# A hybrid FFN and gated-DeltaNet layer on one core: requests, joins and block copies around the first scans in another order

## The reference, cut to what matters

```python
def mix_heads(q, k, v, g, beta, s0):            # per head and direction, per chunk
    a_low = where(strict, einsum(kb, kc) * decay, 0.0)
    sol = triangular_solve(eye + a_low, rhs)    # rhs = [v*beta, k*beta*exp(gc)]
    u_val, w_kd = split(sol)
    def step(S, xs):
        v_new = u_i - w_i @ S
        o = (q_i * exp(g_i)) @ S + qk_i @ v_new
        S = S * exp(g_last) + (k_i * exp(g_last - g_i)).T @ v_new
        return S, o
def pool_mixer(u, w_pool, pool_scale):          # centred window means, a linear map per group
    p = stack([window_mean(u, w) - u for w in (2, 4, 8, 16)])
    return einsum('blgc,gcd->blgd', p, w_pool) * pool_scale
# y = concat([pool_mixer(...), gate(norm(o), z)]) @ w_out
```

## Time and profile before

| | us |
|---|---|
| median of 3 runs (2853.35 to 2856.04) | 2854.99 |
| the profiled execution | 2856.5 |
| its span, first to last instruction | 2854.6 |
| TensorE matmuls busy (98% of the span) | 2799.8 |
| VectorE busy (57%) | 1616.8 |
| ScalarE busy (35%) | 989.9 |
| POOL busy (8%) | 220.8 |

### The profile page before, as it was taken

The page is one execution under the profiler, slowest core; times in us unless marked ns, Lnnn a source line. Parts: engine busy times, 40 slices in busy tenths (PEclk is TensorE's granted clock), DMA queues, the critical chain, the costliest instruction groups (busy, mean ns, idle before and its releaser), DMA issues. The chain is left out here.

```text
span 2854.6 us, 41614 instructions
## 1 busy us (share of the span) xinstructions
PE 2799.8 (98%) x15400; PEld 2357.2 (83%) x15400; DVE 1616.8 (57%) x2080; ACT 989.9 (35%) x1451; POOL 220.8 (8%) x373
## 2 busy tenths in 40 slices
PE   6999999999999999999999999999999999999998
PEld 4688888888888888888888888878988888888887
DVE  4567767677677752223226766745675555555444
ACT  3222222222222221111214555544354444444443
POOL 0000000000000000000101103555120000000001
PEclk9999999999999999999999999999999999999999
DMA  9866677677988956655563666685456666666664
GB/s 369 308 207 221 199 222 221 203 223 250 317 310 304 317 183 201 193 184 171 193 195 97 172 197 182 206 262 171 155 180 191 190 191 191 191 191 192 190 190 144
DMA packets 410340, 604.67 MB, mean 212 GB/s; under 512 B 52960, under 2 KB 303840, under 8 KB 401520
## 3 DMA queue, kind: packets, MB, share of 16 engines
q1 hardware_dynamic: 361824, 419.52, 47.5%
q10 hardware_dynamic: 48400, 183.63, 19.0%
HBM read 560.02 MB, written 43.02 MB: 211 GB/s over the span
## 5 line engine op out<-in xcount | busy, mean ns | idle before, releaser
L2003 DVE TENSOR_TENSOR wl<-raw,wh 128x1024 fp32r<-128x1024 f32 x638 | 784.8, 1231 | 927.2 <-ACT wh L1523 926.5
L1523 ACT CAST wh<-raw 128x1024 fp32r<-128x1024 f32 x638 | 667.7, 1048 | 1455.4 <-PE ps L785 929.9
L783 PE MATMUL ps<-x,wh 128*128 128x512 f32 (+1 forms) x2312 | 903.1, 391 | 0.1
L785 PE MATMUL ps<-x,wl 128*128 128x512 f32 (+1 forms) x2312 | 897.7, 388 | 0.0
L784 PE MATMUL ps<-x,wh 128*128 128x512 f32 (+1 forms) x2312 | 897.6, 388 | 0.0
L783 PEld LDWEIGHTS ps<-x,wh 128*128 128x128 f32 x2312 | 435.0, 188 | 96.1 <-issue 8.9
L785 PEld LDWEIGHTS ps<-x,wl 128*128 128x128 f32 x2312 | 434.7, 188 | 89.9
L784 PEld LDWEIGHTS ps<-x,wh 128*128 128x128 f32 x2312 | 435.1, 188 | 87.3
L2195 DVE SCALAR_TENSOR_TENSOR acc<-abuf,cT,acc 128x1024 f32<-128x1024 f32 x300 | 371.2, 1278 | 19.2 <-DMA abuf<-in_w_ada 18.9
L791 PE MATMUL ps<-x,wh 128*128 128x512 f32 x1408 | 349.2, 393 | 2.6 <-DVE x L2073 2.6
L791 PEld LDWEIGHTS ps<-x,wh 128*128 128x128 f32 x1408 | 254.3, 189 | 48.6 <-issue 2.9
(11 more groups left out here) (309 smaller groups left out, 2346.2 us busy)
## 6 DMA issues: line engine op xcount, KB each, us to landing
raw<-in_ffn_w_in SPq DMA_DIRECT2D x704, 256.0 KB, 3.2
raw<-in_ffn_w_out SPq DMA_DIRECT2D x176, 512.0 KB, 3.6
abuf<-in_w_ada ACTq DMA_DIRECT2D x64, 1024.0 KB, 7.1
abuf<-in_w_ada ACTq DMA_DIRECT2D x96, 512.0 KB, 3.9
x<-d_h ACTq DMA_DIRECT2D x80, 512.0 KB, 3.2
ada_t<-in_ada SPq DMA_DIRECT2D x64, 512.0 KB, 9.3
raw<-in_w_in SPq DMA_DIRECT2D x128, 256.0 KB, 3.5
raw<-in_w_out SPq DMA_DIRECT2D x32, 512.0 KB, 4.5
```

Source lines behind the costliest of these rows:

```text
L783: mm(out, ah, bh, start=first, stop=False, skip_group_check=reopened)
L785: return mm(out, al, bh, start=False, stop=last, skip_group_check=reopened)
L1523: nc.scalar.copy(wh[:, t % HL, :], raw[:, t % RAW, :]).then_inc(hi_done, 1)
L2003: tt(tl, raw[:, t % RAW, :], th.bitcast(F32), ALU.subtract).then_inc(lo_done, 1)
```

## The change

Six things move; no product is added or taken away.

1. SP requests `UF` of head 1 (`level_rows(1)`) ahead of output tiles 0 and 1.
2. In the second pooling set, ScalarE does the join's copy or negation of a step ahead of that step's weight split, and VectorE its negation.
3. In scan 1 VectorE does `fill(0)`, the low part `yl` of pooling group 0, behind `out_mean(0)` and ahead of `state(0)`, where it stood behind `out_gate(0)`.
4. `place` can do its GI half (`"g"`) and its FI half (`"f"`) apart. The GI half ends with a wait for its own copies.
5. `LANE_STEPS` of the second batch has five parts for three: columns 16 to 30 are cut in 16 to 21, 22 to 24 and 25 to 30.
6. POOL's order in the scans: before, columns 16 to 30 came behind `out_power(0)` and ahead of `place(3)`. Now come columns 16 to 21, the GI half of `place(3)`, columns 22 to 24, the FI half, `out_power(1)`, columns 25 to 30. The semaphore `xl_zero` is called `pool_wrote`, and also counts the GI half.

```diff
-LANE_STEPS = (((0, 11), (11, 21), (21, BLK - 1)), ((0, 4), (4, 16), (16, BLK - 1)))
+LANE_STEPS = (((0, 11), (11, 21), (21, BLK - 1)), ((0, 4), (4, 16), (16, 22), (22, 25), (25, BLK - 1)))
...
             set_load(0)
+            level_rows(1)
             out_load(0)
             out_load(1)
-            level_rows(1)
             out_load(2)
...
             for k in range(K_TILES):
-                if k < K_TILES - AHEAD:
-                    split(0, 0, T_POOL + K_TILES + k + AHEAD)
                 if k == 2:
                     copy_y32(0)
...
                 elif k == 5:
                     negate_tn64(0)
+                if k < K_TILES - AHEAD:
+                    split(0, 0, T_POOL + K_TILES + k + AHEAD)
...
                     out_mean(h - 1)
+                    if h == 1:
+                        fill(0)
...
-                fill(0)
+                if h != 1:
+                    fill(0)
                 fill(1)
...
-            def place(h):
+            def place(h, part=None):
...
+                if part == "g":
+                    i.then_inc(pool_wrote, 1)
+                    pool.wait_ge(pool_wrote, 5)
+                    return
                 if h >= 2:
-                    to_g(None, 1)
-                    to_g(1, 0)
                     pool.wait_ge(HS["pe_vn"], at("pe_vn", h - 2, 8))
...
             for h in range(1, HEADS):
-                if h + 1 < HEADS:
+                if h == 2:
+                    place(3, "g")
+                    lanes(1, 3)
+                    place(3, "f")
+                elif h + 1 < HEADS:
                     place(h + 1)
                 out_power(h - 1)
                 if h == 1:
                     lanes(1, 2)
+                elif h == 2:
+                    lanes(1, 4)
```

More of the change, by code:

```diff
@@ L411, in build @@
             sem("yp_hi"), sem("yp_lo"))
-        lt_in, xl_zero, lane_step, lanes_done, fg_out = (
-            sem("lt_in"), sem("xl_zero"), sem("lane_step"), sem("lanes_done"), sem("fg_out"))
+        lt_in, pool_wrote, lane_step, lanes_done, fg_out = (
+            sem("lt_in"), sem("pool_wrote"), sem("lane_step"), sem("lanes_done"), sem("fg_out"))
         set_in = [sem("set_in0"), sem("set_in1")]
@@ L2780, in to_g @@
                         if m is not None:
-                            block_to(GI, b, m)
+                            i = block_to(GI, b, m)
+                    return i
                 def to_f(m_even, m_odd):
@@ L2788, in to_f @@
                     i.then_inc(HS["placed"], 1)
[L2790 to L2797, removed]
+                if part != "f":
+                    pool.wait_ge(HS["level_in"], at("level_in", h, PER["level_in"]))
+                    if h:
+                        pool.wait_ge(HS["pe_tn64"], at("pe_tn64", h - 1, 1))
+                    else:
+                        pool.wait_ge(zeroed, 5)
+                        pool.wait_ge(spilled["q"], 16 * HEADS)
+                        pool.wait_ge(spilled["z"], 16 * HEADS)
+                    to_g(0, None)
+                    if h >= 2:
+                        to_g(None, 1)
+                        i = to_g(1, 0)
+                if part == "g":
+                    i.then_inc(pool_wrote, 1)
+                    pool.wait_ge(pool_wrote, 5)
+                    return
                 if h >= 2:
-                    to_g(None, 1)
-                    to_g(1, 0)
                     pool.wait_ge(HS["pe_vn"], at("pe_vn", h - 2, 8))
@@ L2820, in lanes @@
                         pool.wait_ge(fg_out, FG_DMAS * 16)
[L2821 to L2824, removed]
+                    nc.gpsimd.memset(flat, 0.0).then_inc(pool_wrote, 1)
+                    pool.wait_ge(pool_wrote, 2 * b + 1)
+                    nc.gpsimd.memset(flat[:, 0:BLK * BLK:BLK + 1], 1.0).then_inc(pool_wrote, 1)
+                    pool.wait_ge(pool_wrote, 2 * b + 2)
                 for j in range(lo, hi):
```

## The result

The changed kernel took **2863.36 us** (median of 9 runs, 2860.57 to 2865.60); the kernel before, on the same chip, 2854.99 us (9 runs, 2850.26 to 2856.41). The ratio is 1.0028, with a 95% interval of 1.0019 to 1.0036: slower by 8 us, where 3.8 were forecast and 2852.5 to 2864.0 was the range. Its profiled execution took 2863.61 us, with a span of 2861.8.

What follows compares the result with a forecast made beforehand. TensorE was taken as the bound, with only its idle stretches and clock to win back. The 6.8 us gained are waited away at head 3's set: +1.7 + 2.4 - 0.3 = +3.8, median 2858.8 us, range 2852.5 to 2864.

Steps and rivals of the forecast that it cites:

- the two signs of error: Prediction wrong if XP ends before 1950 us, or if SP issues head 3's set before 1960 us.
- the likeliest case: Whole kernel: 3.8 us slower, median 2858.8 us, counted as the same; given 0.47.
- the start of head 3's scan: TensorE waits for head 3's set until 1972.7 us, 1.7 us later than before; bounds 0 and +5.2.
- g: TensorE's lead at the end of the second scan: 1.1 + 1.6 = 2.7 us, bounds 1.4 and 3.2.
- at most some 1.6: At the second scan's start, POOL's ors of head 0 lets at most some 1.6 us of gain through.
- From the start of ors to XP's end: On POOL, ors of head 1, columns 25 to 30, copy XP: 8.15 us, ending at 1958.7 - g.
- From XP's end to the first product of head 3: On SP, store landing 4.2 us, head 4's eight block loads 3.9, head 3's set 8.6: 16.7 us.
- The low clock: At head 3's scan start, behind TensorE's idle time: costs 2.4 us, bounds 1.2 and 4.5.
- the 0.3 us for scan 4's set: Scan 4's 0.3 us wait for s_z goes, since its set is no longer last to come.
- Rival B: Head 3's set lands slowly (10.8 us), low clock stays long before scan 3: +8.1 us, 2863.1; chance 0.20.
- Rival C: UF's wait only moves to tile 0's cast, g is 1.6, scan 3 later: +4.9 us, 2859.9; chance 0.15.
- Rival A': Hold-up before scan 3 shorter, clock returns at once: 0 to 5.7 us gained, 2849.3 to 2855; chance 0.12.

Runs made afterwards that it cites:

- the placing alone: Kernel before with only POOL's new program (columns 16 to 21, GI, 22 to 24, FI, ors, 25 to 30, XP): 2864.02 us, ratio 1.0030.
- set first, blocks sooner: Changed kernel with head 3's set loaded first on SP, columns recut, tile 0's cast behind the y32 copy, XL stored before XP: 2857.58 us, ratio 1.0007.
- TensorE kept busy: Changed kernel with 42 added, unused products on TensorE ahead of the wait for head 3's set: 2862.04 us, ratio 1.0025.
- the set first: Changed kernel with head 3's set loads ahead of the second batch's stores and head 4's block loads on SP: 2856.47 us, ratio 1.0000.
- edits 1 to 3, columns left out: Kernel before with items 1 to 3 of the change, and columns 10 to 30 of the second batch's substitution left out: 2847.68 us, ratio 0.9971.

## Why the prediction was right in kind and short in size

**The mechanism held, step by step.** The wait before y64 went, L1437 and head 3's join lost theirs, UF's wait gave way to one of 1.27 us for Y behind the cast of tile 0, as the prediction had it. The Trainium skill, "DMA: Bandwidth & Descriptors", section "Queues, rings and completion order", was cited for UF landing no later than tile 0 had: it landed 8.0 us after its issue at 1895.22, which is 21.6 us behind the first join, where tile 0 had landed after 22.8, and the join did not wait: the trace agrees. Scan 3 waited 10.1 us for s_z, at the edge of the 7 to 10 named, and the clock of 0.5 behind it came. Neither of the two signs of error occurred: XP ended at 1959.63, not before 1950, and the set was issued at 1967.82, not before 1960. The experiments place the loss in this chain: the placing alone has all of it, and with SP's order altered it falls to 1.6 us by the medians (2856.47 against 2854.90).

**The verdict missed the likeliest case.** The forecast was 3.8 us and "the same"; measured were 8.4 (5.4 to 10.3 by the interval), slower. The step that came out too small is the start of head 3's scan, forecast at 1972.7 us, "1.7 us **later** than before". Counted from the first join, it was 4.1 us later in the first pair of traces and 5.5 in the second. Three terms were too small in the first trace, all pulling one way:
- g, TensorE's lead at the start of head 2's scan: 2.7 forecast, 2.1 measured (65.8 us behind the first join instead of 67.9). It was not lost at UF: TensorE was 2.7 us ahead at head 1's second join and 3.4 at the start of head 1's scan. POOL's ors of head 0 then let 1.8 of it through to the turning of head 0's output (L1345), near the "at most some 1.6" of the prediction. The wait before L1437 went on top, 2.9 us ahead, but the low clock behind the new wait for o, which the sum has no term for, took 0.7 back by head 2's y64 join.
- From the start of ors to XP's end: 8.15 us priced from the earlier trace rows, 9.15 measured. One of the twelve column instructions takes 1.20 us, where its like of before took 0.33.
- From XP's end to the first product of head 3: 16.7 us priced, 17.5 measured (18.6 in the second trace).

These make 0.6 + 1.0 + 0.8 us, the missing 2.3 to rounding (93.2 us behind the first join forecast, 95.5 measured). Such an extra of 0.9 us on one POOL instruction is in the trace of before too, elsewhere: three copies of head 3's placing took 1.97 us at 1947.92, and three of the same size 0.96 at 1951.59. The low clock was over-priced (2.4, measured 1.6 to 1.7), and the 0.3 us for scan 4's set came back (0.5 measured). So the forecast's own terms, put right by the first pair of traces, give 4.1 + 1.7 - 0.5 = 5.3 us. The other 3 us of the measured 8.4 are in no term of it, and their cause is open.

**Rival B had the time but half the cause.** It gave 2863.1 by a slow landing and a low clock of over 6 us under work. Its first condition came, a start of scan 3 later than 1974.5 (1977.09), though not by the landing alone: that of s_z, 6.8 and 7.9 us after issue, lay between the 6.3 and 8.5 of the earlier trace rows. Its second did not: the low clock under TensorE's work was short, under 4 us. Rival C described the UF edit rightly (the wait did move to the cast), but its smaller g doesn't hang on the cast: with the cast out of Y's way (set first, blocks sooner) head 2's scan started no sooner than in the changed kernel, 67.1 and 65.8 us behind the first join. Rival A' called for a price under the lowest row, and none came.

**What the range did.** It held the result only by its upper end, 0.6 us inside, and with 3 us of the loss unexplained that is partly luck. The prices were each taken near the middle or the kind end of their rows, from a single trace, and the two traces of before differ by 1.7 us in where head 3's scan starts.

## What to carry to other kernels

When a step is moved back on an engine that works in order, follow what its last product feeds through every queue behind it: here a copy that TensorE never waits for directly held up, by way of SP's order, a transfer that did not need it. A wait in a profile is not a gain to be had until it is known which engine sets the next meeting point; two traces of the same kernel showed the idle time once at UF and once at POOL's blocks, with nearly the same total. A chain of many links is better priced from two traces than from one.

## What was not expected of the hardware

- Single POOL instructions take 0.9 us more than their like. Some fall on the same instruction in every trace with the same order: tm of 87 elements took 1.20 us in the changed kernel, in it again, with the placing only, with TensorE kept busy and with the set first, and 0.33 before. Others move by an instruction or two between two traces of one program (columns of 240 elements in the first trace of the changed kernel, of 231 in the second). The cause is open.
- XL's store of 512 KB landed 3.8 us after its issue when the last of the set's six loads had been issued 3.5 us before it, and 7.5 us when that load was issued 0.5 us before it.
- The low clock moves with the idle time. It followed UF's wait in one execution of before (0.50 from 1908 to 1916 us) and POOL's wait in the other (0.50 from 1928 to 1938). With the waits mostly gone (edits 1 to 3, columns left out; 2845.59 us, one of its faster executions) the granted clock was 1.00 from 1900 to 1990 us, and the time from the first join to the end was 964 us.
